# A spare buffer of 8 rows made 2 rows: the buffers behind it move by 96 bytes

## The chip, the cores and the metric

The kernel runs on one core of a Trainium2 chip. The metric is the device time of one execution in microseconds (us). Before the change the median of three runs is 2823.58 us (2823.52 to 2824.51).

## The reference

A one-layer encoder trunk over 512 tokens of width 2048, in float32. The mixers (attention A, an RWKV-7 recurrence B, sliding attention C) share one input projection; a cross-attention into 256 memory tokens and a squared-ReLU MLP of width 8192 follow.

```python
proj = rms_norm(h) @ w_in
h = h + concat([A(proj), B(proj), C(proj)]) @ w_out
q = rms_norm(h) @ x_wq;  k, v = rms_norm(mem) @ x_wk, rms_norm(mem) @ x_wv
h = h + softmax(q k^T * 128**-0.5) v @ x_wo
h = h + square(relu(rms_norm(h) @ mlp_w1)) @ mlp_w2
out = rms_norm(h)
```

## The kernel before

Every large product is computed as three float32r matmuls, high by high, low by high and high by low (`split_mm`, L1075 to L1077). Weights stream in units of 128 x 768 or 128 x 1024 into `w_raw` (four slots); ScalarE rounds a unit into `w_hi` (L416), VectorE subtracts to get `w_lo` (L695), and TensorE uses both. A product either holds the weights still and streams the activation ("w", 128 weights by 512 or 256 activation columns), or holds the activation still and streams the weights ("a"). Semaphores written out by hand set the order on each engine; no scheduler decides anything.

The stages follow each other: norm of x (`x_mix`), eight RWKV pairs with attention projections around them (main loop over `g` and `u`; the small 64 x 64 float32 products all go through `both`, L1102), cross keys and values from the memory tokens with the chunk attention beside them, the output projections, the cross attention, and eight MLP chunks. In an MLP chunk the first half streams `act_hi`/`act_lo` over still weights into PSUM, which become `mid_hi` (ScalarE, L660) and `mid_lo` (VectorE, L1038); the second half holds `mid_hi`/`mid_lo` still and streams weights.

`rq` is a small table of per-token factors. Row 0 is written at L995 and read at L633 and L1009, row 1 is written at L1050 and read at L959. Rows 2 to 7 are never touched.

SBUF buffers are placed by a stack allocator: each begins where the last one ended, rounded up to 32 bytes. First come the buffers of the whole program (`top`): `act_hi`, `act_lo`, `w_raw`, `w_hi`, `w_lo`, `ident`, `gain`, `diag`, `ssq`, `tiny`, `rms`, and `rq` as the last. Three layouts (`lay1`: `x_mix`; `lay2`: the RWKV buffers; `lay3`: `h`, `mid_hi`, `mid_lo`, attention, cross attention and MLP) are then laid over each other, all starting right behind `rq`. Within a layout the offsets from its start depend on the sizes before them: `g_pad` of `lay2` is 2080 bytes, so what stands behind it is 32 bytes off from what stands before it.

Of the kernel before, what the change touches and what calls it, by code (L numbers as in the profile page):

```python
# [23 lines left out]
P = 128  # L24
SEQ, D, N_MEM, D_FF = 512, 2048, 256, 8192
TT = SEQ // P
# [36 lines left out]
def hybrid_layer(nc, x, mem, gains, w_lora, w_pairs, w_rest, pair_prm, fin_prm, gup_tail, lora_mu,  # L63
                 a_line, c_line, sinks, norm_final, out):
    top = ExitStack()
    with top:
        def alloc(stack):
            return lambda name, shape, dt=F32: stack.enter_context(nc.sbuf_tensor(name, shape, dt))
# [4 lines left out]
        sb = alloc(top)  # L73
# [9 lines left out]
        ssq = sb("ssq", [P, TT, 4])  # L83
        tiny = sb("tiny", [P, 1])
        rms = sb("rms", [P, 8])
        rq = sb("rq", [P, 8, TT])
        ps = top.enter_context(nc.psum_tensor("ps", [P, 8, 512], F32))
        scr_y = nc.dram_tensor("scr_y", (PAIRS, P, SEQ), F32).ap()
        scr_qkv = nc.dram_tensor("scr_qkv", (QKV // 3, 3, P, SEQ), F32).ap()
# [1437 lines left out]
```

## Time and profile before

| | |
|---|---|
| median of three runs | 2823.58 us (2823.52 to 2824.51) |
| the profiled execution | 2823.58 us, its span 2821.8 us |
| TensorE busy | 2740.1 us (97%), 18532 matmuls |
| VectorE, ScalarE, GpSimd busy | 1194.6, 824.6, 123.0 us |
| granted TensorE clock, mean | 0.994 |
| moved by DMA | 249.25 MB, 88 GB/s over the span |

The span runs from the first to the last instruction of the profiled execution. Busy shares are averages over stages; the chain that ended last says which engine the end waited for. Matmuls are pipelined, so a matmul's own duration (391 ns for 512 columns) is longer than the distance between two starts, and the distance is what counts.

### The profile page before, as it was taken

How to read it: one execution, taken by the hardware profiler on the slowest of the kernel's cores; microseconds unless marked ns; L12 is line 12 of the kernel's file. 1: busy time of each engine (PE TensorE's matmuls, PEld its weight loads, DVE VectorE, ACT ScalarE, POOL GpSimd, SP SyncE). 2: the span in 40 equal slices, each digit the busy share in tenths (PEclk: the TensorE clock that was granted, in tenths of full speed). 3: DMA queues.
4: the chain of work that ended last, by engine and by line, in shares of the span. 5: the costliest groups of instructions: out<-in, count | busy, mean ns of one | idle time of the engine just before them, and what ended most of it. 6: DMA issues, size and time to landing. Idle time of an engine off the chain costs nothing.

```text
span 2821.8 us, 44631 instructions
## 1 busy us (share of the span) xinstructions
PE 2740.1 (97%) x18532; PEld 2180.1 (77%) x18532; DVE 1194.6 (42%) x1838; ACT 824.6 (29%) x1358; POOL 123.0 (4%) x238
## 2 busy tenths in 40 slices
PE   7999999999999999998899999999999999999997
PEld 6777777777767766786688888888888888888885
DVE  3245566566523554444433333233432333324333
ACT  3222222222223544344422131221312222122232
POOL 3000010111112011000000000000000000000000
PEclk9999999999999999999999999999999999999998
DMA  3321111111125432221123332323232322322333
GB/s 130 107 80 48 47 47 46 49 51 47 55 85 184 158 103 76 68 90 60 61 96 97 97 97 91 103 96 96 91 100 96 96 96 96 97 96 97 97 97 112
DMA packets 71470, 249.25 MB, mean 88 GB/s; under 512 B 8784, under 2 KB 8912, under 8 KB 69408
## 3 DMA queue, kind: packets, MB, share of 16 engines
q1 hardware_dynamic: 64512, 222.59, 24.5%
q0 software_dynamic: 6816, 24.60, 2.7%
q8 instruction: 110, 1.80, 0.3%
q14 instruction: 32, 0.26, 0.0%
HBM read 236.93 MB, written 10.22 MB: 88 GB/s over the span
## 4 chain that ended last, share of the span: by engine, by line
PE 93%; DVE 4%; ACT 1%; issue 1%; DMA 1%; DVEq 0%; POOL 0%; SPq 0%; ACTq 0%
PE ps L1075 27%; PE ps L1077 25%; PE ps L1076 25%; PE ps L1102 9%; PE ps L1310 1%; PE ps L1289 1%; PE ps L1081 1%; PE ps L1298 1%; PE ps L1096 0%; DVE w_lo L695 0%; ACT pad L416 0%; ACT w_hi L416 0%; DMA h<-in_mem 0%; DMA x_mix<-in_x 0%; DVE h L953 0%
## 5 line engine op out<-in xcount | busy, mean ns | idle before, releaser
L695 DVE TENSOR_TENSOR w_lo<-w_raw,w_hi 128x1024 fp32r<-128x1024 f32 (+2 forms) x440 | 505.1, 1149 | 1222.8 <-ACT w_hi L416 1222.5
L416 ACT ACTIVATE w_hi<-w_raw 128x1024 fp32r<-128x1024 f32 (+2 forms) x440 | 438.9, 999 | 1517.2 <-PE ps L1077 1517.1
L1075 PE MATMUL ps<-act_hi,w_hi 128*128 128x512 f32 x1792 | 731.6, 408 | 10.3 <-ACT pad L416 4.7
L1077 PE MATMUL ps<-act_hi,w_lo 128*128 128x512 f32 x1792 | 701.1, 391 | 0.0
L1076 PE MATMUL ps<-act_lo,w_hi 128*128 128x512 f32 x1792 | 700.1, 391 | 0.0
L1075 PE MATMUL ps<-w_hi,mid_hi 128*128 128x512 f32 x1088 | 425.8, 391 | 8.1 <-DVE act_lo L732 6.7
L1076 PE MATMUL ps<-w_lo,mid_hi 128*128 128x512 f32 x1088 | 424.4, 390 | 0.0
L1077 PE MATMUL ps<-w_hi,mid_lo 128*128 128x512 f32 x1088 | 424.3, 390 | 0.0
L1075 PEld LDWEIGHTS ps<-act_hi,w_hi 128*128 128x128 f32 x1792 | 336.8, 188 | 105.1 <-issue 18.0
L1077 PEld LDWEIGHTS ps<-act_hi,w_lo 128*128 128x128 f32 x1792 | 336.9, 188 | 72.5
L1076 PEld LDWEIGHTS ps<-act_lo,w_hi 128*128 128x128 f32 x1792 | 337.3, 188 | 68.4 <-issue 5.8
L1075 PEld LDWEIGHTS ps<-w_hi,mid_hi 128*128 128x128 f32 x1088 | 204.9, 188 | 51.3 <-issue 7.4
L1077 PEld LDWEIGHTS ps<-w_hi,mid_lo 128*128 128x128 f32 x1088 | 204.9, 188 | 42.8
L1076 PEld LDWEIGHTS ps<-w_lo,mid_hi 128*128 128x128 f32 x1088 | 205.0, 188 | 42.0
L959 DVE SCALAR_TENSOR_TENSOR h<-ps,rq,h 128x512 f32<-128x512 f32 x128 | 87.2, 744 | 104.9 <-PE ps L1077 104.9
L1075 PE MATMUL ps<-w_hi,act_hi 128*128 128x512 f32 x256 | 106.2, 415 | 4.2 <-DVE h L953 3.6
L1077 PE MATMUL ps<-w_hi,act_lo 128*128 128x512 f32 x256 | 100.3, 392 | 0.0
L1076 PE MATMUL ps<-w_lo,act_hi 128*128 128x512 f32 x256 | 100.1, 391 | 0.0
L410 POOL DMA_DIRECT2D w_raw<-in_norm_final x1 | 0.5, 533 | 1629.7 <-DVE w_lo L695 1629.7
L1075 PEld LDWEIGHTS ps<-w_hi,act_hi 128*128 128x128 f32 x256 | 48.0, 187 | 21.4 <-issue 13.3
L1077 PEld LDWEIGHTS ps<-w_hi,act_lo 128*128 128x128 f32 x256 | 48.0, 188 | 10.8
L1076 PEld LDWEIGHTS ps<-w_lo,act_hi 128*128 128x128 f32 x256 | 48.2, 188 | 8.1
(268 smaller groups left out, 2443.0 us busy)
## 6 DMA issues: line engine op xcount, KB each, us to landing
w_raw<-in_w_rest SPq DMA_DIRECT2D x320, 512.0 KB, 3.6
w_raw<-in_w_pairs SPq DMA_DIRECT2D x112, 384.0 KB, 3.0
x_mix<-in_x SPq DMA_DIRECT2D x4, 1024.0 KB, 8.1
qk<-scr_qkv POOLq DMA_DIRECT2D x16, 256.0 KB, 3.1
h<-in_x POOLq DMA_DIRECT2D x4, 1024.0 KB, 11.3
out<-h SPq DMA_DIRECT2D x4, 1024.0 KB, 4.3
scr_qkv<-pad POOLq DMA_DIRECT2D x15, 256.0 KB, 2.8
w_raw<-in_w_lora SPq DMA_DIRECT2D x8, 288.0 KB, 7.4
```

Of the source, the lines that this page charges most:

```text
L410: pool.dma_start(gain_out, norm_final.to_broadcast([P, D])).then_inc(s["gout_in"], 16)
L416: return nc.scalar.activation(dst, src, ACT.Copy, scale=scale)
L695: V.tensor_tensor(dst, w_raw[:, slot, 0:dst.shape[-1]], high.bitcast(F32), ALU.subtract).then_inc(s["w_split"], 1)
L959: V.scalar_tensor_tensor(dst, bank(4 * par + t), rq[:, 1, t:t + 1], dst, ALU.mult, ALU.add).then_inc(s["bank_evac"], 1)
L1075: mm(dst, a_hi, b_hi, start=start, stop=False)
L1076: mm(dst, a_hi, b_lo, start=False, stop=False)
L1077: return mm(dst, a_lo, b_hi, start=False, stop=stop)
L1081: last = mm(ps[:, b, t * P:(t + 1) * P], src[:, t, kt * P:(kt + 1) * P], diag[:, t, :], start=True, stop=True)
L1102: last = mm(dst[hf], lhsT[hf], rhs[hf], start=start, stop=stop)
L1289: mm(ps[:, 4 + n % 2, 0:keys], qk[hf, t % 2, 0, i * P:(i + 1) * P], qk[hf, t % 2, 1, key0:key0 + keys], start=True, stop=True).then_inc(s[ ...
L1298: last = nc.tensor.transpose(ps[:, 6, b * P:(b + 1) * P], att_p[:, n % 4, b * P:(b + 1) * P], ident[:, :])
L1310: last = mm(ps[HALF[half], 7, i * P:(i + 1) * P], vt[:, key0 // P + b, v0:v0 + L], att_pT[:, n % 2, b * P:(b + 1) * P], start=b == 0, stop ...
```

## The change

`rq` is declared with 2 rows of 4 floats where it had 8. It takes 32 bytes of each partition, not 128. No instruction is added, taken away or moved: the order on all five engines is the same, row for row.

```diff
         tiny = sb("tiny", [P, 1])
         rms = sb("rms", [P, 8])
-        rq = sb("rq", [P, 8, TT])
+        rq = sb("rq", [P, 2, TT])
         ps = top.enter_context(nc.psum_tensor("ps", [P, 8, 512], F32))
```

What changes is addresses. `rq` starts at byte 119,808 of a partition before and after. The three layouts start at 119,936 before and at 119,840 after, and every buffer of `lay1`, `lay2` and `lay3` lies 96 bytes lower. By the place of a buffer's start modulo 64:

| buffers | before | after |
|---|---|---|
| all of `top` (`act_hi`, `act_lo`, `w_raw`, `w_hi`, `w_lo`, `ident`, ...; `rms` is at 32) | 0 | 0 (unmoved) |
| `lay1`: `x_mix` | 0 | 32 |
| `lay2` up to `g_pad`: `r_s`, `k_s`, `v_s`, `sig_w`, `a_gate`, `cum_sig`; and `prm2`, `gup2`, `lora`, `pad1` | 0 | 32 |
| `lay2` from `g_inv` to `fprm`, without `prm2`: `kk_norm`, `k_mod`, `k_dec`, `m_ab`, `inv`, `y_raw`, `y_cent`, `r_dec`, `a_dec`, `b_tok`, `k_tok`, `v_tok`, `invT`, `state`, ...; and `eye2`, `ones2`, `mean2`, the masks, `pad0`, `pad2` | 32 | 0 |
| all of `lay3`: `h`, `mid_hi`, `mid_lo`, `xk_t`, `xq_t`, `qk`, `vt`, `att_p`, `x_p`, `relu_t`, `sq_t`, ... | 0 | 32 |

## Rows read from the trace of the kernel before

**Rows 1.** The page: span, and busy time by engine.

```profile
span 2821.8 us, 44631 instructions
PE 2740.1 (97%) x18532; PEld 2180.1 (77%) x18532; DVE 1194.6 (42%) x1838; ACT 824.6 (29%) x1358; POOL 123.0 (4%) x238
```

**Rows 2.** The page: chain that ended last, shares by engine and line.

```profile
PE 93%; DVE 4%; ACT 1%; issue 1%; DMA 1%; DVEq 0%; POOL 0%; SPq 0%; ACTq 0%
PE ps L1075 27%; PE ps L1077 25%; PE ps L1076 25%; PE ps L1102 9%; PE ps L1310 1%; PE ps L1289 1%; PE ps L1081 1%; PE ps L1298 1%; PE ps L1096 0%; DVE w_lo L695 0%; ACT pad L416 0%; ACT w_hi L416 0%; DMA h<-in_mem 0%; DMA x_mix<-in_x 0%; DVE h L953 0%
```

**Rows 3.** Busy time by stretch; columns in the first line, us.

```profile
core 0: us, PE busy (x) PEld busy (x) DVE busy (x) ACT busy (x) POOL busy (x), PEclk, DMA share, GB/s
...
171.00:866.00 695.00, 684.40 (x9132) 513.70 (x9129) 397.24 (x601) 187.87 (x371) 64.17 (x70) 1.00 0.18 54
...
1400.00:2805.00 1405.00, 1399.38 (x6174) 1157.89 (x6172) 487.48 (x527) 359.34 (x428) 0.53 (x1) 1.00 0.29 95
```

**Rows 4.** TensorE in order of time, MLP: start us, us, engine, line, operation.

```profile
1500.12 0.39 PE L1077 MATMUL ps<-w_hi,mid_lo 128*128 128x512 f32 x1
1500.34 0.39 PE L1075 MATMUL ps<-w_hi,mid_hi 128*128 128x512 f32 x1
...
1504.88 0.39 PE L1077 MATMUL ps<-w_hi,mid_lo 128*128 128x512 f32 x1
```

**Rows 5.** The same view, cross-attention keys, 256 columns each.

```profile
930.05 0.28 PE L1076 MATMUL ps<-mid_lo,w_hi 128*128 128x256 f32 x1
...
931.24 0.28 PE L1077 MATMUL ps<-mid_hi,w_lo 128*128 128x256 f32 x1
```

**Rows 6.** Groups by line and shape, TensorE weight loads: count | busy us, mean ns.

```profile
L1075 PEld LDWEIGHTS ps<-act_hi,w_hi 128*128 128x128 f32 x1792 | 336.8, 188 | 105.1 <-issue 18.0 <-ACT pad L416 6.7 <-DVE act_lo L732 3.7
L1075 PEld LDWEIGHTS ps<-w_hi,mid_hi 128*128 128x128 f32 x1088 | 204.9, 188 | 51.3 <-issue 7.4 <-DVE mid_lo L1021 1.6
L1102 PEld LDWEIGHTS ps<-eye,k_dec 64*64 64x64 f32 x256 | 8.1, 135 | 0.4 <-issue 0.4
L1102 PEld LDWEIGHTS ps<-eye,a_gate 64*64 64x64 f32 x256 | 8.1, 135 | 0.4 <-issue 0.4
```

**Rows 7.** TensorE in order of time, one RWKV pair, runs of 32.

```profile
267.22 1.10 PE L1102 MATMUL ps<-r_dec,k_dec 64*64 64x64 f32 x32
270.12 1.10 PE L1102 MATMUL ps<-a_gate,a_dec 64*64 64x64 f32 x32
271.06 1.10 PE L1102 MATMUL ps<-a_dec,a_gate 64*64 64x64 f32 x32
```

**Rows 8.** Groups by line and shape, VectorE.

```profile
L777 DVE TENSOR_TENSOR r_s<-pad 128x512 f32<-128x512 f32 x8 | 5.5, 682 | 0.0
L812 DVE TENSOR_TENSOR k_dec<-k_mod,g_inv 128x512 f32<-128x512 f32 x8 | 5.5, 685 | 0.0
L813 DVE TENSOR_TENSOR r_dec<-r_s,g_pad 128x512 f32<-128x512 f32 x8 | 5.5, 685 | 0.0
L1038 DVE TENSOR_TENSOR mid_lo<-sq_t,mid_hi 128x512 fp32r<-128x512 f32 x64 | 44.3, 692 | 3.3
```

**Rows 9.** Groups by line and shape, ScalarE.

```profile
L416 ACT ACTIVATE act_hi<-ps 128x512 fp32r<-128x512 f32 x8 | 4.8, 599 | 6.1 <-PE ps L1310 6.1
L416 ACT ACTIVATE b_tok<-ps 128x512 f32<-128x512 f32 x8 | 4.8, 599 | 8.8 <-PE ps L1102 8.8
L416 ACT ACTIVATE pad<-ps 128x512 f32<-128x512 f32 x45 | 23.7, 600 | 70.5 <-PE ps L1077 70.5
```

**Rows 10.** Chain that ended last, in order: start us, us, what.

```profile
2.21 11.13 DMA x_mix<-in_x
866.62 11.24 DMA h<-in_mem
```

**Rows 11.** The page, DMA issues: size, median us to landing.

```profile
x_mix<-in_x SPq DMA_DIRECT2D x4, 1024.0 KB, 8.1
out<-h SPq DMA_DIRECT2D x4, 1024.0 KB, 4.3
```

## The prediction

> **What bounds the kernel now.** I read the page's busy shares first. TensorE is busy for 2740.1 of 2821.8 us, VectorE for 1194.6 and ScalarE for 824.6 [rows 1]. The chain that ended last says the same: 93% of it is TensorE, and 77% the three matmul lines of the split products [rows 2]. So a microsecond counts only if it lengthens TensorE's stream, or lies at the few places where TensorE waits. The stretches show where there is room. In the MLP, 1405 us, TensorE is busy for 1399.38 us, so 5.6 us are left open in it; the RWKV stretch of 695 us has 684.40 us busy and 10.6 us open [rows 3]. Here TensorE's own rate is the time, and the granted clock is at full speed (1.00, the 2.4 GHz level) in both.
>
> **The change part by part.** Nothing is removed, added or moved: the same instructions with the same waits. `rq` keeps its start, and its reads (L633, L959, L1009) and writes keep their shapes. Six rows that nobody touched are gone. What is left is the shift of three layouts by 96 bytes. Buffers that started at a multiple of 64 now start 32 past one, and many RWKV buffers the other way round. The question is whether any engine or DMA has another rate at the one place than at the other. I go through the users, each time looking for rows of before that already hold both placements.
>
> *VectorE and ScalarE.* L812 reads and writes buffers that all lie at 32: 685 ns. L777 writes `r_s` at 0 and reads `pad` at its start and one element (4 bytes) past it: 682 ns. L813 mixes `r_s` at 0, `r_dec` at 32, and `g_pad`, whose chunks step by 65 elements and so start anywhere: 685 ns [rows 8]. L1038, in the MLP, has everything at 0 and takes 692 ns, which is not less. ScalarE's copies out of PSUM take 599 ns into `act_hi` (0), 599 ns into `b_tok` (32) and 600 ns into `pad` (4 bytes past either) [rows 9]. So 32 against 0 costs these engines at most 3 ns in 685, and by these rows nothing. What would hide a difference there is TensorE's stream: VectorE is busy for 487.48 us of the MLP's 1405 [rows 3]. If the cover were gone, 3 ns on each of the 1838 VectorE instructions would be 5.5 us; I take 0.
>
> *TensorE, the small float32 products.* Three kinds stand in one stretch. With moving `r_dec` at 32 and still `k_dec` at 32 the run of 32 records takes 1.10 us; with moving `a_gate` at 0 and still `a_dec` at 32, 1.10 us; with moving `a_dec` at 32 and still `a_gate` at 0, 1.10 us [rows 7]. Weight loads take 135 ns from `k_dec` (32) and 135 ns from `a_gate` (0) [rows 6]. Placement does not show, on either side of the product. After the change these buffers change places. A resolution of 0.01 us in 1.10 is 0.9%, so from these rows alone the stretch of 684.40 busy us is fixed to 0.9%, or 6 us to either side; the row with the mean, 135 and 135 ns over 256 records each, is the closer one. I take 0.
>
> *TensorE, the float32r products.* This is the part that no row settles, because every float32r operand of the kernel before starts at a multiple of 64. After the change `act_*` and `w_*` still do, and only `mid_hi` and `mid_lo` don't. They are held still in 3 x 1088 = 3264 matmuls [rows 6] (cross-attention output and the MLP's second half), and streamed in 3 x 144 = 432 (cross keys and values, a part of the queries). For the held side the distance of two starts in the MLP is (1504.88 - 1500.12)/21 = 226.7 ns [rows 4]. With 256 columns, ten matmuls later, it is (931.24 - 930.05)/10 = 119 ns [rows 5], with a still operand of the same size. So 256 columns cost 107.7 ns, 512 cost 215.4, and 11.3 ns of a matmul are not columns. A weight load finishes inside 119 ns there without holding the stream up any further; under 512 columns it has some 107 ns of room. Were the row's 128 x 4 = 512 bytes fetched in pieces of 64, the shifted row would touch 9 and not 8, and the load of 188 ns [rows 6] would grow by an eighth, 23.5 ns: hidden in that room. For the streamed side the same picture gives 33 pieces instead of 32 for 512 columns, or 17 for 16; one piece is 16 columns, 6.7 ns, and 432 x 6.7 ns = 2.9 us. That picture is mine and no row shows pieces. The bounds: at the lower end 0, since the float32 products show no gain or loss in either direction; at the upper end the 11.3 ns that are not columns come twice in each of the 3264, which is 36.9 us. Between these ends the nearest rows are the float32 products of the same engine, which show nothing, so I take 0.
>
> *DMA.* The transfers into moved buffers that stand on the chain are the tokens, 11.13 us, and the memory tokens, 11.24 us [rows 10]; the stores of `h` land 4.3 us after issue each [rows 11], and only the last is open at the end. The weights, nearly all the traffic, go to `w_raw`, which does not move. No large transfer of before goes to a place at 32, so the bounds are 0 and, if the row's 8192 bytes were to be written at half the rate, 11.1 + 11.2 + 4.3 = 26.6 us. For reading SBUF there is something nearer: L777's `pad`, 4 bytes past its start, is also what the projections are stored from, and nobody waits for that. I take 0.
>
> The store of `h` reads rows of 8192 bytes that began at 128 past a multiple of 256 and begin at 32 past one now. The Trainium skill (DMA: Bandwidth & Descriptors, How a descriptor splits into AXI transactions) says that a descriptor off a 256-byte boundary starts its first transaction at the boundary below and pays for the bytes before it. By that rule a row cost 8 + 31 x 8 + 4 = 260 beats before, and costs 8 + 31 x 8 + 1 = 257 now, an estimated 1% less. The sum would be some 0.05 us lower (1% of the last store), which changes nothing in it; the trace of before cannot tell the two placements apart.
>
> **The sum.** 0 on VectorE and ScalarE, 0 on the float32 products, 0 on the float32r products, 0 on the transfers. The profiled execution took 2823.58 us, 1.8 us more than its span, and it is the median of the three runs too, so no correction lies between them. The forecast is 2823.6 us, no change. A measurement of this kernel can tell a difference of about 0.2%, 5.6 us, from none.
>
> **The rivals.**
> - *Slower: a still float32r operand off 64 bytes stretches the seam between matmuls.* Place: cross-attention output and the second half of each MLP chunk, where TensorE has no idle time to hide it. Price up to 3264 x 11.3 ns = 36.9 us, giving 2860 us; it decides once it is over 5.6 us / 3264 = 1.7 ns per matmul, four cycles. For it: nothing in the trace excludes it, and the stream is full there [rows 4]. Against it: the load has 107 ns of room, and float32 loads don't care. Chance 8%.
> - *Slower: transfers to places at 32 lose rate.* 26.6 us at most, 2850 us; at a quarter lost, 6.7 us. For it: these loads stand on the chain [rows 10]. Against it: the rows in SBUF are 8192 bytes long, and only their two ends are touched otherwise. Chance 4%.
> - *Faster: the RWKV buffers gain.* `g_inv` and nearly all that stands behind it come to a multiple of 64. At the 0.9% that the rounding leaves open, 6 us: 2817.5 us. Against it: `a_gate` lies at 0 already and its loads and products are not faster [rows 6, 7]. Chance 5%.
> - *Engines collide differently in SBUF*, since the layouts stand otherwise against `act_*` and `w_*`. One percent of the time in which VectorE runs (1194.6 us [rows 1]) is 12 us if all of it reached TensorE; most of it would not. Either sign, under 5.6 us nearly always. Chance 3% beyond it, two thirds of that slower.
> - *That the change does nothing to addresses* (the start rounded up to 64 or more) is excluded: the starts are 119,936 and 119,840.
>
> **How the numbers follow.** The forecast has 80%; the rivals have 8, 4, 5 and 3%. From them: faster by over 0.2%, 5 + 1 = 6%; slower, 8 + 4 + 2 = 14%; that leaves 80% for within 0.2%. The range goes to 2818 us below, the gaining rival's end, and to 2832 us above, which takes in the small streamed term of 2.9 us, a quarter lost on the transfers and a stretched seam of up to 2.6 ns; the tail up to 2860 us stays outside with under 10%.
>
> **What would show it.** If right, the profile after shows the distance of two starts in an MLP chunk's second half at 226.7 ns and with 256 columns at 119 ns, weight loads from `mid_*` at 188 ns, runs of 32 small products at 1.10 us, the first transfer at about 11.1 us, and VectorE's 512-element instructions at 682 to 693 ns, all within rounding. The forecast is wrong if the MLP stretch is over 1405 us by more than its 5.6 us, or if TensorE's busy time is off 2740.1 us by as much. A distance that grew only in the second halves points at the still operand; one that grew only at the cross keys, at the streamed one; an x load that lands later, at the transfers.

## The result, and the profile after

The changed kernel takes 2845.78 us (median of four runs, 2844.33 to 2847.59) against 2824.05 us before: ratio 1.0078, 95% interval 1.0061 to 1.0093, 21.7 us slower. The forecast was no change, 2823.6 us, with a range from 2818 to 2832 us. It was wrong.

The page of the profiled execution (2847.2 us), where it answers to [rows 1]: TensorE's busy time grew by 23.5 us, VectorE's and ScalarE's moved by 0.1 and 0.6 us.

```profile
span 2845.5 us, 44631 instructions
PE 2763.6 (97%) x18532; PEld 2181.3 (77%) x18532; DVE 1194.5 (42%) x1838; ACT 825.2 (29%) x1358; POOL 123.5 (4%) x238
```

By stretch (columns in the first line), to be read against [rows 3]. The RWKV stretch ends where it did; the MLP needs 1429 us where it needed 1405, and TensorE fills it as before. From the second chunk on, an MLP first half takes 86.9 us from its first start to its last (86.8 before) and a second half 89.4 us (86.8 before).

```profile
core 0: us, PE busy (x) PEld busy (x) DVE busy (x) ACT busy (x) POOL busy (x), PEclk, DMA share, GB/s
...
171.00:866.00 695.00, 684.42 (x9130) 513.55 (x9127) 397.04 (x601) 188.30 (x371) 63.97 (x70) 1.00 0.17 54
...
1400.00:2829.00 1429.00, 1423.04 (x6182) 1160.19 (x6180) 487.79 (x527) 360.86 (x430) 0.53 (x1) 1.00 0.28 93
```

TensorE in order of time in a second half (start us, us, engine, line, operation). From the first row to the last are 21 matmuls: 4.90 us, 233.3 ns apart, where it was 226.7 ns [rows 4]. 3264 matmuls x 6.6 ns are 21.5 us, and the medians differ by 21.7 us. The profiled execution is 23.6 us over that of before; most of the other 2 us is the first MLP half, 91.7 us against 90.4, which experiment 5 does not repeat (90.1 us).

```profile
1519.64 0.40 PE L1076 MATMUL ps<-w_lo,mid_hi 128*128 128x512 f32 x1
...
1524.54 0.40 PE L1076 MATMUL ps<-w_lo,mid_hi 128*128 128x512 f32 x1
```

Groups by line and shape (count | busy us, mean ns), first two rows of the kernel before, then the kernel after. The matmul with `mid_hi` held and `w_lo` streamed takes 400 ns where it took 390. The one with `mid_lo` streamed at 512 columns in the queries grew as well, to 396 ns from 389, though there are only 48 products of that kind. The weight load's own record stays at 188 ns [rows 6]: that row does not show the loss. VectorE is as in [rows 8].

```profile
L1076 PE MATMUL ps<-w_lo,mid_hi 128*128 128x512 f32 x1088 | 424.4, 390 | 0.0
L1076 PE MATMUL ps<-mid_lo,w_hi 128*128 128x512 f32 x16 | 6.2, 389 | 0.0
```

```profile
L1076 PE MATMUL ps<-w_lo,mid_hi 128*128 128x512 f32 x1088 | 435.1, 400 | 0.0
L1075 PEld LDWEIGHTS ps<-w_hi,mid_hi 128*128 128x128 f32 x1088 | 205.1, 188 | 61.7 <-issue 7.5 <-DVE mid_lo L1021 1.6
L1076 PE MATMUL ps<-mid_lo,w_hi 128*128 128x512 f32 x16 | 6.3, 396 | 0.0
L777 DVE TENSOR_TENSOR r_s<-pad 128x512 f32<-128x512 f32 x8 | 5.5, 682 | 0.0
L812 DVE TENSOR_TENSOR k_dec<-k_mod,g_inv 128x512 f32<-128x512 f32 x8 | 5.5, 684 | 0.0
```

The small float32 products, against [rows 7]: unchanged at 1.10 us a run, although their buffers moved as well.

```profile
267.46 1.10 PE L1102 MATMUL ps<-r_dec,k_dec 64*64 64x64 f32 x32
270.37 1.10 PE L1102 MATMUL ps<-a_gate,a_dec 64*64 64x64 f32 x32
```

The cross keys, 256 columns: (931.53 - 930.34)/10 = 119 ns, as in [rows 5], although `mid_*` is streamed there from its new place.

```profile
930.34 0.28 PE L1076 MATMUL ps<-mid_lo,w_hi 128*128 128x256 f32 x1
...
931.53 0.28 PE L1077 MATMUL ps<-mid_hi,w_lo 128*128 128x256 f32 x1
```

The two transfers on the chain, against [rows 10]: 11.12 and 11.32 us.

```profile
2.22 11.12 DMA x_mix<-in_x
...
866.93 11.32 DMA h<-in_mem
```

### The profile page after: what moved, and what is told of

It is laid out like the page before. It is cut to its first block, busy times and chain, and to the rows that moved or that the text cites. A ratio compares the mean times of both kernels' runs of the same rounds, so it can differ in the third digit from the quotient of the medians.

```text
span 2845.5 us, 44631 instructions
## 1 busy us (share of the span) xinstructions
PE 2763.6 (97%) x18532; PEld 2181.3 (77%) x18532; DVE 1194.5 (42%) x1838; ACT 825.2 (29%) x1358; POOL 123.5 (4%) x238
## 4 chain that ended last, share of the span: by engine, by line
PE 93%; DVE 3%; ACT 1%; issue 1%; DMA 1%; DVEq 0%; POOL 0%; SPq 0%; ACTq 0%
PE ps L1075 27%; PE ps L1076 25%; PE ps L1077 25%; PE ps L1102 8%; PE ps L1310 1%; PE ps L1289 1%; PE ps L1081 1%; PE ps L1298 1%; PE ps L1096 0%; DVE w_lo L695 0%; ACT pad L416 0%; ACT w_hi L416 0%; DMA h<-in_mem 0%; DMA x_mix<-in_x 0%; DVE h L953 0%
## 5 line engine op out<-in xcount | busy, mean ns | idle before, releaser
L1076 PE MATMUL ps<-w_lo,mid_hi 128*128 128x512 f32 x1088 | 435.1, 400 | 0.0
```

Of the source, the lines that this page charges most:

```text
L1076: mm(dst, a_hi, b_lo, start=False, stop=False)
```

## The experiments

From here on a buffer's place is its start modulo 256 bytes, and the distance of a product is the place of its held operand minus that of its streamed one, again modulo 256. A pair such as (32, 0) gives the two places, the held operand's first. Two operands are in step when their distance is 0. `act_*` and `w_*` start at 128 in the kernel before, and so do `mid_*`: distance 0. The change puts `mid_*` at 32: where they are held and the weights streamed, the distance is 160. The prediction never forms that distance; the table in the section on the change speaks of places modulo 64 only. Two theories stood at the start: *own address* (a float32r operand off a multiple of 64 costs time by itself) and *pair* (the place of the held operand against the streamed one is what counts). In the fences of TensorE rows below, 21 matmuls lie from the first start of a pair of rows to the second.

**1. The address alone.** `rq` stays small, 96 unused bytes follow it.

```diff
         rq = sb("rq", [P, 2, TT])
+        sb("spacer", [P, 24])
```

> The changed kernel with 96 unused bytes behind rq, so that the three layouts start where they did before (119,936). Address theory: the whole loss is the address of what lies behind rq, so 2824 us, distance between matmul starts in an MLP second half 226.7 ns. Rival (something in the declaration of rq itself, its own span, matters): 2845.8 us, 233.3 ns.

Measured: 2824.25 us, ratio 1.0003 (0.9993 to 1.0012). The distance of starts is 4.76/21 = 226.7 ns again. With the old addresses behind `rq` the whole loss is gone, so the size of `rq` itself costs nothing.

```profile
1519.77 0.39 PE L1078 MATMUL ps<-w_hi,mid_lo 128*128 128x512 f32 x1
...
1524.53 0.39 PE L1078 MATMUL ps<-w_hi,mid_lo 128*128 128x512 f32 x1
```

**2. A multiple of 64, not of 128.**

```diff
-        rq = sb("rq", [P, 2, TT])
+        rq = sb("rq", [P, 4, TT])
```

> rq with 4 rows: the layouts start at 119,872, a multiple of 64 but not of 128 (before they started at a multiple of 128). If the period that counts is 64 bytes: 2824 us and 226.7 ns. If it is 128 or more: some 2846 us and 233.3 ns.

Measured: 2831.66 us, ratio 1.0025 (1.0015 to 1.0036); 4.81/21 = 229.0 ns. This is neither of the two numbers that were expected, but a third of the loss. A yes-or-no rule about 64 or 128 bytes cannot give a third, so the quantity has more than two values.

```profile
1519.62 0.39 PE L1077 MATMUL ps<-w_hi,mid_lo 128*128 128x512 f32 x1
...
1524.43 0.39 PE L1077 MATMUL ps<-w_hi,mid_lo 128*128 128x512 f32 x1
```

**3. Everything off a multiple of 64, in step.**

```diff
+        sb("spacer", [P, 8])
         act_hi = sb("act_hi", [P, KT, SEQ], F32R)
```

> The kernel before with 32 unused bytes ahead of act_hi: act, w and mid all start 32 past a multiple of 64, still and streamed operands alike. Own-address theory (an operand off a multiple of 64 costs 6.7 ns in a 512-column matmul, whatever the other one does): nearly all of the 9408 + 48 x 3 or so 512-column float32r matmuls pay, at least 9408 x 6.67 ns = 62.8 us, 2887 us; if both operands pay apart, 2950 us. Pair theory (a still and a streamed operand at different places modulo 64 disturb each other): all are in step again, 2824 us.

Measured: 2824.07 us, ratio 1.0000 (0.9991 to 1.0010), 226.7 ns. The own-address theory is refuted for a place 32 off: every float32r operand lies there and nothing is lost.

```profile
1519.81 0.39 PE L1077 MATMUL ps<-w_lo,mid_hi 128*128 128x512 f32 x1
...
1524.57 0.39 PE L1077 MATMUL ps<-w_lo,mid_hi 128*128 128x512 f32 x1
```

**4. A probe of the disputed cost by itself.** It has only a load of x, copies into float32r and float32 tiles, and 31 blocks of 48 matmuls, and ran once. It does not compute the reference. The core of it:

```python
for i in range(COUNT):   # COUNT = 48
    mm(ps[:, i % 8, 0:n], st[:, so + (i % 4) * P:so + (i % 4 + 1) * P],
       mv[:, mo + (i % 2) * n:mo + (i % 2 + 1) * n], start=True, stop=True)
```

> Leaves the reference's computation out. 31 blocks of 48 matmuls, 128 weights held still, 512, 384 or 256 columns streamed, each block with the still operand and the streamed one at chosen bytes past a multiple of 64; read is the distance between starts. Own-address theory: 226.7 ns at (0, 0), 233.3 at (32, 0) and (0, 32) and no less at (32, 32), no loss at 64 and 128. Pair theory: 226.7 at (0, 0), (32, 32), (16, 16), (48, 48), 233.3 wherever the two differ modulo 64. With 256 columns both expect about 119 ns at (0, 32), as in the trace after; for the still operand at 32 with 256 columns own-address theory expects 126 ns or, if room under the stream hides it, 119. Float32: no difference.

Busy time by stretch; each stretch runs from a block's first start to the next block's, 48 distances (the count in brackets also takes in what reaches over an edge). In order: (held, streamed) at (0, 0), (32, 0), (0, 32), (32, 32).

```profile
core 0: us, PE busy (x), PEclk, DMA share, GB/s
53.76:64.64 10.88, 10.88 (x49) 1.00 0.00 0
75.53:86.72 11.19, 11.19 (x50) 1.00 0.00 0
142.63:153.84 11.21, 11.21 (x50) 1.00 0.00 0
187.06:197.98 10.92, 10.92 (x49) 1.00 0.00 0
```

Divided by 48: 226.7, 233.1, 233.5 and 227.5 ns. Shifting either operand by 32 costs 6.4 and 6.8 ns, shifting both costs nothing (inside the last block, away from its edges, the distance of starts is 226.8 ns); no other engine was at work, so no collision with VectorE, ScalarE or a DMA is needed. Two expectations failed. 64 and 128 bytes on the held side are not free (233.3 and 232.5 ns), and 16 and 48 bytes on both sides gave 230.0 ns, not 226.7: at these places, which no buffer of the kernel has, being in step is not enough. Float32 operands showed 429 ns between records in all three placements. The loss also hangs on the columns: with 384 streamed columns (0, 0), (32, 0) and (0, 32) all gave 173.3 ns, and with 256 the two shifted placements were faster than (0, 0), 118.2 and 116.7 against 119.8 ns.

**5. `mid_*` alone.** The kernel before, with `mid_*` at its new place and all else at the old.

```diff
+        s3("spacer", [P, 40])
         mid_hi = s3("mid_hi", [P, FT, SEQ], F32R)
         mid_lo = s3("mid_lo", [P, FT, SEQ], F32R)
+        s3("spacer2", [P, 24])
```

> The kernel before with 160 unused bytes ahead of mid_hi and 96 behind mid_lo: mid_hi and mid_lo stand modulo 256 where the change put them, everything else where it was before. Pair theory (the weight load's reads and the stream's reads collide by their distance modulo 256): the whole loss, 3264 x 6.7 ns = 21.9 us, 2846 us, 233.3 ns between starts. Rival (other moved buffers, h, relu_t, the RWKV ones, carry a part): less than 2846 us.

Measured: 2847.00 us, ratio 1.0078 (1.0061 to 1.0095), 4.90/21 = 233.3 ns. `mid_hi` and `mid_lo`, two of the many moved buffers, carry the whole loss.

```profile
1519.79 0.39 PE L1077 MATMUL ps<-w_hi,mid_hi 128*128 128x512 f32 x1
...
1524.69 0.39 PE L1077 MATMUL ps<-w_hi,mid_hi 128*128 128x512 f32 x1
```

**6. The weights follow.** The changed kernel, with `w_hi` and `w_lo` moved into step with `mid_*`, out of step with `act_*`.

```diff
+        sb("spacer", [P, 40])
         w_hi = sb("w_hi", [P, SPLIT_W], F32R)
         w_lo = sb("w_lo", [P, SPLIT_W], F32R)
+        sb("spacer2", [P, 24])
```

> The changed kernel with w_hi and w_lo moved by 160 bytes (modulo 256), so that they are in step with mid again and out of step with act, which does not move. Pair theory: the MLP's second halves go back to 226.7 ns, and all products of w with act pay, 3 x (1792 + 256) = 6144 of them, 6.7 ns each, 41 us over the kernel before: some 2865 us, with 233.3 ns in the MLP's first halves. Own-address theory, already against the all-moved run: both halves at 233.3 ns or more, 2885 us and up.

Measured: 2854.91 us, ratio 1.0105 (1.0088 to 1.0122). The loss changes sides, as only the pair theory has it. In a second half (first two rows) 4.76/21 = 226.7 ns, in a first half (last two) 4.89/21 = 232.9 ns, although `act_*` never moved. The size was overrated: some 30 us over the kernel before, not 41. The eight first halves lost their 8 x 2.6 = 21 us, but all before the MLP lost 11.5 us (its first product starts at 1417.9 us, not 1406.4), half of the 20.5 us that 3072 products at 6.7 ns would be. What is missing is missing in the RWKV stretch: taken by the start of the same matmul in both traces, the 576 products ahead of it lost 5.1 us, its own 1452 lost only 0.8 us, and those behind it 5.6 us. In that stretch these products stand between waits and small float32 products; that this is why they lose so little was not tested.

```profile
1519.75 0.39 PE L1077 MATMUL ps<-w_hi,mid_hi 128*128 128x512 f32 x1
...
1524.51 0.39 PE L1077 MATMUL ps<-w_hi,mid_hi 128*128 128x512 f32 x1
...
1649.77 0.39 PE L1077 MATMUL ps<-act_hi,w_hi 128*128 128x512 f32 x1
...
1654.66 0.39 PE L1077 MATMUL ps<-act_hi,w_hi 128*128 128x512 f32 x1
```

**7. The roundest address.**

```diff
-        rq = sb("rq", [P, 8, TT])
+        rq = sb("rq", [P, 16, TT])
```

> rq with 16 rows: the layouts start at 120,064, a multiple of 256, the roundest address of all runs, but 128 from the place of w and act modulo 256. Alignment theory (round addresses are good): 2824 us. Pair theory by distance, with the first probe's 232.4 ns at a distance of 128: 3264 x 5.7 ns = 18.6 us more, 2842 us.

Measured: 2842.25 us, ratio 1.0060 (1.0043 to 1.0077), 4.87/21 = 231.9 ns. Layouts that start at a multiple of 256 are 17 us slower than those of the kernel before, which start 128 past one, since `mid_*` now stand 128 from the weights. The first probe's 232.4 ns had given this time ahead of the run.

```profile
1519.81 0.39 PE L1077 MATMUL ps<-w_hi,mid_lo 128*128 128x512 f32 x1
...
1524.68 0.39 PE L1077 MATMUL ps<-w_hi,mid_lo 128*128 128x512 f32 x1
```

**8. The curve.** The second probe, run once, lets the held operand run behind the streamed one's place.

```diff
-                    last = mm(ps[:, i % 8, 0:n], st[...], mv[...], start=True, stop=True)
+                    at = so + (i % 4) * P
+                    last = mm(ps[0:cols, i % 8, 0:n], still[:, at:at + cols],
+                              moving[:, mo + (i % 2) * n:mo + (i % 2 + 1) * n], start=True, stop=True)
```

> Leaves the reference's computation out. 42 blocks of 48 float32r matmuls on an otherwise idle core: the still operand 0 to 512 bytes behind the streamed one's place in steps of 32, then common shifts, narrower still operands and fewer streamed columns. Pair theory: 226.7 ns at 0, 256 and 512, a repeating curve between them (233 at 32 to 160, 229 at 192), the same distance gives the same time wherever both stand, and with 64 or 32 weights the loss shrinks, since the load reads less. If the period is longer than 256, the curve from 256 to 512 differs. Own-address theory: no dependence on the streamed operand's place.

Stretches of 48 distances, in order: held 96, 128, 160, 192 and 256 bytes behind; then (160, 64), a distance of 96; then (0, 0) with 64 weights instead of 128; then 256 columns at a distance of 0 and of 64.

```profile
core 0: us, PE busy (x), PEclk, DMA share, GB/s
74.75:85.98 11.23, 11.23 (x49) 1.00 0.01 1
85.98:97.14 11.16, 11.16 (x49) 1.00 0.00 0
97.14:108.34 11.20, 11.20 (x49) 1.00 0.00 0
108.34:119.34 11.00, 11.00 (x50) 1.00 0.01 1
130.53:141.42 10.89, 10.89 (x49) 1.00 0.00 0
241.70:252.93 11.23, 11.23 (x49) 1.00 0.00 0
252.93:263.98 11.05, 11.05 (x50) 1.00 0.01 1
319.58:325.32 5.74, 5.74 (x49) 1.00 0.01 3
325.32:330.98 5.66, 5.66 (x51) 1.00 0.00 0
```

Divided by 48: 234.0, 232.5, 233.3, 229.2, 226.9; 234.0; 230.2; 119.6 and 117.9 ns. The distance of 96 gives the same time at two places, 256 is as good as 0, and the six distances tried from 288 to 512 repeated those from 32 to 256 within 0.2 ns. Three of its values can be held against runs of the full kernel: 160 (233.3, the change 233.3), 192 (229.2, experiment 2 229.0), 128 (232.5, experiment 7 231.9). Two things came otherwise: with half the weights the loss shrinks as expected (231.5 ns at a distance of 96), but from a time at distance 0 that has risen to 230.2 ns, and with 256 columns a distance of 64 is 2 ns better than none.

**9. Which two reads?** The third probe, run once, alternates the places from matmul to matmul.

```diff
-            for so, mo, n, cols in tests:
+            for offsets, n, cols, kind in tests:
+                    so, mo = offsets[i % len(offsets)]
```

> Leaves the reference's computation out. Blocks of 48 matmuls as in the second probe. In two kinds of block the offsets alternate: (0, 0), (96, 96) keeps each product's two operands in step, but then the weights loaded under a running stream are out of step with that stream; (96, 0), (0, 96) does the reverse. Load theory (the loss comes from the next weights' load against the stream that runs meanwhile): the first kind 233 ns or more, the second 226.7 ns. Own-pair theory (the loss comes from something between a product's own two operands): the other way round. Still offsets of 16 to 240 in between: no distance below 226.7 ns if 0 is the best place; one below it would be worth nearly 9400 matmuls times the difference. bfloat16 operands: no loss if the rate of reading matters, the same 6.7 ns if only places do.

Stretches of 48 distances, in order: (0, 0), (96, 96); then (96, 0), (0, 96); then 128 columns at distance 0; then bfloat16 with 512 columns at distances 0 and 96.

```profile
core 0: us, PE busy (x), PEclk, DMA share, GB/s
45.27:56.50 11.23, 11.23 (x50) 1.00 0.00 0
56.50:67.53 11.03, 11.03 (x49) 1.00 0.01 1
245.41:250.71 5.30, 5.30 (x49) 1.00 0.00 0
311.60:321.97 10.37, 10.37 (x49) 1.00 0.01 2
321.97:332.33 10.36, 10.36 (x49) 1.00 0.00 0
```

Divided by 48: 234.0, 229.8; 110.4; 216.0, 215.8 ns. The first kind costs as much as being out of step everywhere, though each product is in step with itself, so own-pair theory fails. But the second kind should have been 226.7 by the load theory and is 229.8. With 160 bytes in place of 96 the two kinds gave the same (234.0 and 230.2), with 32 bytes the reverse order (231.9 and 233.3). So the load theory has the order right in two cases of three and the 226.7 ns in none: it is not shown. With 128 columns the stream should take a quarter of 512 columns, and 110 ns pass; 192 columns take no longer (112 ns inside either block), so the columns do not set the distance there. That the weight load does is my reading. bfloat16 takes no notice of the places 0, 32 and 96. No offset tried, 16 to 240, went below 226.7 ns at 512 columns.

## Why the prediction was wrong

- *What bounds the kernel*: right. TensorE's stream was the time, and the loss appeared there one for one.
- *VectorE, ScalarE, small float32 products, transfers, 0 each*: right. The two transfers moved by 0.01 and 0.08 us, the RWKV stretch's TensorE time by 0.02 us, VectorE's busy time by 0.1 us and ScalarE's by 0.6 of 825 us, off the chain. The test was sound where rows of before held both placements.
- *Float32r products, 0*: this step failed, and it is a mis-sized term. Its bounds were 0 and 36.9 us (11.3 ns in 3264 matmuls); the measured value is 6.6 ns in 3264, 21.5 us, 58% of the way up. I took the lower end because "the nearest rows are the float32 products of the same engine". They are no neighbours: at 512 columns float32 has 429 ns between records and bfloat16 216 ns, and neither changed with the places tried; float32r, at 226.7 ns, does.
- *"A weight load finishes inside 119 ns ... under 512 columns it has some 107 ns of room"*: the load does fit (110 ns from start to start at 128 columns, load included), and the room did not help: 6.6 ns came all the same, while the load's own record stayed at 188 ns, without the 23.5 ns of the prediction's picture. The picture of 64-byte pieces is gone on both sides: experiment 3 has every row in 9 pieces and loses nothing, and of the 432 streamed matmuls, priced at 2.9 us, the 384 with 256 columns lost nothing.
- *The question itself* was set too narrow: "another rate at the one place than at the other". I looked up each buffer's own place modulo 64, where the kernel before had hidden the variable: all float32r operands stood at distance 0 from each other, so no row could show what a distance costs. That every one of them did was itself to be seen in the addresses, and was the warning.
- *The rival* "a still float32r operand off 64 bytes stretches the seam" (the part of the distance that is not columns) had place, sign and bound right (8%, up to 2860 us) and the cause wrong: experiment 3 puts all of them off 64 and loses nothing. The range's end counted 2.6 ns for it; 6.6 came.
- The rule on descriptors was weighed for 0.05 us. The last store landed after 4.3 us as before, so it could not be tested.

What stays open is the mechanism: which accesses meet, if it is accesses that do. Shown are that at 512 columns and places at multiples of 32 the time follows the distance modulo 256 of held and streamed operand, that of the three types tried float32r alone does so, and that no other engine is needed. The Trainium skill (SBUF — State Buffer, Who interferes with whom) gives TensorE two independent read ports, one for the streamed operand and one for the weight load, and lets only the pair shared by VectorE and GpSimd cause contention; taken at its word, no placement of TensorE's operands should matter. The runs differ from that by 6.6 ns a matmul, and the measurement decides.

## What to carry to other kernels

A declaration that frees memory moves everything allocated behind it. When TensorE streams 512 columns of float32r back to back, keep all held and streamed buffers of neighbouring products at the same place modulo 256 bytes, on a multiple of 32 (a spacer restores it); pairs that are in step each by itself but alternate between two places still cost up to 7.3 ns (experiment 9). Give round addresses no credit by themselves. Before taking 0 for an unseen placement, ask whether the rows that show no effect vary the thing that changes: here they varied a buffer's place and never the distance between two float32r operands. And after any edit of sizes, compare addresses as well as instructions.

## What the runs showed that I had not expected

- The distance's cost is not smooth: 0 ns at 0, 6.6 to 7.7 at 32 to 96, 5.8 at 128, 6.7 at 160, 2.2 at 192, 6.6 at 224, 0 at 256. A distance of 16 bytes gave 226.7 ns in the first probe and 233.4 in the third, whose streamed slices alternate every second matmul and not every one; the order of slices may count too, which was not tested by itself.
- The cost needs a long stream, as far as it was tried. With 384 columns a distance of 32, 96 or 224 costs nothing and one of 160 costs 3.4 ns; with 480 columns 96 costs 3.3 ns.
- With 256 columns the best distance is not 0: 116.7 ns at 224, 117.4 at 96 and 117.9 at 64, against 119.8. The kernel has 384 such products, 1.2 us at most by the best of these. Experiment 2 puts them at 64: from the first start to the last they took 96.0 us, 97.1 before, too little to see in the kernel's time.
- The kernel before is already at the best place found for 512 columns; no run of the full kernel beat it.
